# Transposing the normalized tiles by DMA from SBUF to SBUF instead of on TensorE, in a hybrid decoder trunk on eight cores

## The reference, cut to what matters

```
h    = rms_norm(x, norm_mix)                       # (B, S, 1024)
proj = h @ w_in                                    # 1024 -> 8192: b_a c_a u_a u_p q_x g_a g_p g_x
y_a  = (b_a * causal_dwconv3(c_a * u_a)) @ w_conv_out
y_p  = per_group_linear(trailing_mean(u_p; 2, 4, 8, 16) - u_p) * pool_scale
mem_n = rms_norm(mem, norm_mem)                    # 256 memory tokens
y_x  = cross_attention(q_x, mem_n @ w_kv) @ w_xattn_out
x    = x + (sigmoid(g_a)*y_a + sigmoid(g_p)*y_p + sigmoid(g_x)*y_x) @ w_out
h    = rms_norm(x, norm_ffn)
x    = x + (silu(h @ w_gate) * (h @ w_up)) @ w_down    # 1024 -> 2816 -> 1024
return rms_norm(x, norm_final)
```

## Time and profile before

| | us |
|---|---|
| median of 3 runs | 1241.22 (1235.62 to 1244.12) |
| span of the profiled execution, slowest core (core 5) | 1244.8 |
| the other cores of that execution | 1225.2 to 1235.6 |
| TensorE busy, of that span | 1166.6 (94%) |
| VectorE, ScalarE busy | 512.5 (41%), 298.8 (24%) |

### The profile page before, as it was taken

How to read it: one execution, slowest core, us unless ns; L and a number is a source line. 1 busy time by engine, 2 the same in 40 slices (tenths; PEclk the granted TensorE clock), 3 DMA queues, 4 the chain that set the end, 5 groups by cost and what they waited for, 6 DMA issues and landing times.

```text
span 1244.8 us, 14721 instructions; the slowest of 8 cores (1225.2 to 1244.8 us)
## 1 busy us (share of the span) xinstructions
PE 1166.6 (94%) x5720; PEld 536.8 (43%) x5720; DVE 512.5 (41%) x504; ACT 298.8 (24%) x412; POOL 132.0 (11%) x154
## 2 busy tenths in 40 slices
PE   2786999999999899999989999989999989999997
PEld 2342444444444444444444444434444444444443
DVE  4003679843334411211163378883333531121125
ACT  5322232211112511001164322221111341101112
POOL 2021111110010210021100001111101021002000
PEclk9988999999999999999989999999999999999999
DMA  9999655535468496059984355557554669009302
GB/s 241 133 133 127 84 68 68 68 43 67 63 83 203 71 145 81 1 86 135 144 212 114 46 68 68 68 68 86 63 63 60 172 99 171 10 1 138 40 17 119
DMA packets 164756, 115.95 MB, mean 93 GB/s; under 512 B 11456, under 2 KB 151872, under 8 KB 164688
## 3 DMA queue, kind: packets, MB, share of 16 engines
q0 software_dynamic: 156640, 85.50, 56.6%
q1 hardware_dynamic: 8048, 29.51, 6.7%
HBM read 192.10 MB, written 8.39 MB: 161 GB/s over the span
## 4 chain that ended last, share of the span: by engine, by line
PE 74%; DVE 10%; DMA 9%; issue 3%; ACT 2%; POOL 0%; another core or an unknown queue 0%; SPq 0%; DVEq 0%; ACTq 0%; POOLq 0%
PE ps L183 74%; DMA ring<-w_kv 4%; DMA ring<-w_in 3%; DVE rden L559 2%; DMA tmp<-x 1%; DMA arena<-x 1%; DVE tmp L475 1%; DVE tmp L478 1%; DVE tmp L509 1%; DVE tmp L513 1%; DVE tmp L468 1%; DVE arena L520 1%; DVE tmp L505 1%; ACT junk L263 1%; PE ps L278 1%
## 5 line engine op out<-in xcount | busy, mean ns | idle before, releaser
L183 PE MATMUL ps<-arena,ring 128*128 128x512 bf16 (+1 forms) x4160 | 878.8, 371 | 33.1 <-DMA ring<-w_in 18.4
L183 PEld LDWEIGHTS ps<-arena,ring 128*128 128x128 bf16 x4160 | 393.1, 98 | 510.0 <-issue 49.2
L719 DVE TENSOR_TENSOR arena<-ps,tmp 128x1024 bf16<-128x1024 f32 x44 | 53.9, 1224 | 254.5 <-PE ps L183 239.6
L183 PE MATMUL ps<-arena 128*128 128x512 bf16 x704 | 155.1, 382 | 1.6 <-DVE stat L267 1.6
L716 ACT ACTIVATE tmp<-ps 128x1024 f32<-128x1024 f32 x44 | 45.1, 1024 | 319.1 <-PE ps L183 319.0
L183 PEld LDWEIGHTS ps<-arena 128*128 128x128 bf16 x704 | 69.0, 98 | 85.1 <-issue 4.1
L176 POOL DMA_DIRECT2D ring<-w_in x64 | 56.0, 875 | 460.0 <-PE ps L183 409.9
L737 DVE TENSOR_TENSOR arena<-ps,arena 128x1024 f32<-128x1024 f32 x32 | 39.2, 1223 | 79.2 <-PE ps L183 79.2
L183 PE MATMUL ps<-ring,arena 128*128 128x512 bf16 x256 | 56.9, 379 | 0.0
L263 ACT ACTIVATE junk<-arena 128x1024 bf16<-128x1024 f32 x40 | 42.1, 1053 | 58.1 <-DVE stat L267 29.0
L559 DVE RECIPROCAL rden<-ps 128x512 f32<-128x512 f32 x16 | 53.6, 3348 | 0.1
(11 more groups left out here) (73 smaller groups left out, 619.7 us busy)
## 6 DMA issues: line engine op xcount, KB each, us to landing
ring<-w_in POOLq DMA_DIRECT2D x64, 512.0 KB, 9.1
arena<-w_down POOLq DMA_DIRECT2D x4, 2816.0 KB, 23.4
ring<-w_gate POOLq DMA_DIRECT2D x20, 512.0 KB, 23.4
ring<-w_up POOLq DMA_DIRECT2D x20, 512.0 KB, 22.7
arena<-x SPq DMA_DIRECT2D x4, 2048.0 KB, 13.4
out<-tmp SPq DMA_DIRECT2D x16, 512.0 KB, 2.8
arena<-x SPq DMA_DIRECT2D x8, 512.0 KB, 15.2
ring<-w_kv POOLq DMA_DIRECT2D x8, 512.0 KB, 43.9
```

The source lines that it names most:

```text
L183: ins = e.matmul(o, l, r, start=s0, stop=s1)
L719: dve(lambda e, u=u, sg=sg, c=c: e.tensor_tensor(out=actT[:, c, :], in0=PU[u][:, 0:TM], in1=sg[:, 0:TM], op=ALU.mult), reads=[("PU", u), ( ...
```

## The change

`transpose_tile` issues one DMA transpose from the norm's buffer `hb` to `hT` (or `memT`) on SyncE's queue. The TensorE transposes, the PSUM buffer that they took from the rotation of three, and the copies out of PSUM are gone. The places in program order of all 35 calls stay. `on_dve` no longer has an effect.

```diff
     def transpose_tile(src_bf, src_keys, rows, dstT, c0, dst_keys, on_dve=False):
-        m = next_pu()
-
-        def fn(e):
-            ins = None
-            for kc in range(KC):
-                ins = e.transpose(PTv[m][:, kc, 0:rows], src_bf[:rows, kc * P:(kc + 1) * P], ident[:rows, :rows])
-            return ins
-        plan.op("pe", fn, reads=src_keys + [("ident",)], writes=[("PU", m)])
-        if on_dve:
-            dve(lambda e: e.tensor_copy(out=dstT[:, :, c0:c0 + rows], in_=PTv[m][:, :, 0:rows]),
-                reads=[("PU", m)], writes=dst_keys)
-        else:
-            act(lambda e: e.activation(out=dstT[:, :, c0:c0 + rows], in_=PTv[m][:, :, 0:rows], func=AF.Copy),
-                reads=[("PU", m)], writes=dst_keys)
+        plan.op("sp", lambda e: e.dma_start_transpose(out=dstT[:, :, c0:c0 + rows], in_=src_bf[:rows, :]),
+                reads=src_keys, writes=dst_keys, dma=True)
```

## The result

The changed kernel takes **1309.98 us**, median of 4 runs (1308.29 to 1325.54), against 1240.4 us before (4 runs, 1235.62 to 1244.12): the ratio is 1.0594, with a 95% interval of 1.0525 to 1.0663. It is 70 us slower. The forecast was 1269 us in a range of 1240 to 1340: the direction and the range held, the size did not, +70 us where +28 was said. In the profile the slowest core (core 2) spans 1307.0 us, and the cores agree (1292.3 to 1307.0). Some executions of every version, the kernel before included, run longer while one die or both show a lower granted clock; ratios, medians and profiles here are of the others.

The account below looks back on a forecast made before the run. TensorE was taken as the bound almost everywhere, full DMA engines at the start. Startup 15, C streams 8.4 and A stream 4.9 sum to +28.3: 1273 against the profiled 1244.8, 1269 us as run median, range 1240 to 1340.

Parts of the forecast that it names:

- Direction and bound: Whole kernel: TensorE, busy 94%, bounds it almost everywhere except the DMA-full start; the change makes it slower, chance 0.75.
- The rival on the other side: C and A stream ends: freed TensorE goes straight on, 18.6 us less, 1223 us; chance 0.03.
- A tile alone: A transpose with nothing beside it lands in 2.8 us: 1.3 fixed plus 1.5 of engine time.
- C streams, +4.2 each: Each C stream's end: last tile lands in 7 us beside weight loads, +2.4, and lower clock after idling, +1.8.
- Startup, +15: Startup: 10.1 tiles at 1.5 us of engine time delay weight loads on full DMA engines, +15 us.
- A stream, +4.9: A stream of half 1: VectorE waits for `hb`, +3.4; last two tiles stand behind a store on SP, +1.5.
- Rival 3: Beside weight loads, 64 pieces per engine wait 0.7 us each: startup, C and A streams +109, 1350 us; chance 0.14.
- Rival 1: Transposes go nearly free: startup costs 0 to 7.5, C ends gain 1.6 each, 1246 us; chance 0.20.
- Rival 4: Everywhere, a tile's eight blocks go one after another, 10.4 us a tile: +218, 1459 us; chance 0.08.

Follow-up runs that it names:

- e1: Kernel before, with only the 16 tiles of the two C streams transposed by DMA: 1282.5 us, ratio 1.0319.
- e5: e1 with the first `w_down` load of each half held until the last transpose has landed: 1243.3 us, ratio 1.0011.
- e2: Kernel before, with only the 9 startup tiles and two memory tiles transposed by DMA: 1256.5 us, ratio 1.0113.
- e9: e3 with five `hb` buffers instead of four: 1246.4 us, ratio 1.0036.
- e3: Kernel before, with only the 8 tiles of the A stream of half 1 transposed by DMA: 1248.8 us (two runs), no ratio.
- e10: e2 with the first `w_kv` load held until all tiles of hT have landed: 1252.6 us, ratio 1.0086.
- e11: Kernel before, with the first seven tiles of each C stream by DMA and the `w_down` load held until the seventh has landed: 1242.7 us, ratio 1.0001.
- e7: e1 with the DMA transpose replaced by a plain copy of the tile in 256-byte pieces: 1284.5 us, ratio 1.0327.
- e8: e1 with the DMA transpose replaced by a plain copy in 2 KB rows to spare buffers: 1250.8 us, ratio 1.0074.

## Why the prediction was wrong, point by point

**Direction and bound: right.** TensorE was freed of 23.0 us and gained nothing from it, because each place ends with a hand-over, not with TensorE. The rival on the other side (1223 us) needed landings that no place had.

**A tile alone: right.** 2.8 us of landing was said; 2.7 to 2.8 us was measured in every quiet moment (e1, e5).

**C streams, +4.2 each: the step that failed,** measured +20.7 and +18.4. Two things in it were wrong. I took 7 us for the landing of the last tile as a value between 2.8 and 16.8, reading the x and gain loads by their bytes. But they go in rows of 4 KB, 8 packets per engine to 512 KB, and a tile goes in 66, of which 64 are of 256 bytes; where queues take turns packet by packet, a number of packets is what has to be carried over, not a size. And I followed the last tile alone ("the first seven tiles are transposed while the DMA engines are nearly idle"). The `w_down` load came out at 427.16 and the seventh tile at 427.6, so it met the flood (19.1 us), and the last tile stood behind it and behind a gain load in the same queue: it landed 24.2 us after its issue where 7 were said, and TensorE idled 26.5 us where 9 were said. The clock was part of it about as said, 1.5 us instead of 1.8; the row that the 1.8 came from stands behind two waits of 3.12 and 1.65 us, though, and not behind a long idle.

**Startup, +15: about the right size for the wrong reason,** +19.6 measured, +16.7 alone. The term was engine time of 1.5 us a tile that delays weights. e2 shows no wait for weights at all: hT is complete at 72 us, not near 60, and sets everything after it. The price of a tile there was 4.9 us in turns with weights, where I had 3 to 4. The engine time itself was 1.16 us with nothing beside it and 2.3 us as a mean over the kernel, where I had 1.5 for all. That +15 lies near +19.6 is luck.

**A stream, +4.9: half of it,** +10.3 measured. Both mechanisms were there (e9): VectorE's wait for `hb`, 4.9 us instead of 3.4, and the end behind the last stores, 5.7 instead of 1.5. The second holds some 2.6 us of lower clock (e3), which I had counted for the C streams only.

**The rivals.** Rival 3 (every small piece waits its turn, 0.14) had the mechanism, and the 66 packets per engine are its 64 pieces and two more. It had the price of a turn from the x loads, 0.7 us; for a piece of 256 bytes a turn took 0.21 us beside `w_down` and 0.07 beside other weights. Hence its +32 us per C stream stood against +20.7 and its +35 at the startup against +19.6. Rival 1 (nearly free, 0.20) is what e5 makes of the C streams. Rival 4, with 10.4 us for every tile, is refuted by the landings of 2.7 us. The Trainium skill ("VectorE: DVE Perf Modes", "The three transpose paths") gives 1309 ns for one block by DMA; the estimate of 10.5 us a tile, which took it eight times, does not hold here: the eight blocks of a tile landed together in 2.7 us. A single block was not run.

**What stays open.** In what order x, mem, weights and transposes would have to be issued for a startup that hides eight transposes wasn't tried beyond e10. Why a tile issued as the flood starts moves hardly a packet in the first microseconds is not shown. And e3, with two times, shows its +10.6 us by its stages only.

## What to carry to other kernels

A small DMA issued beside a running bulk load costs, in the main, its number of packets per engine times the turn of the other queue's packet, not its bytes: count the pieces of both, and look at what is issued in the microseconds around it and ahead of it in its own queue. Where a hand-over must be by DMA, hold the bulk load back until it has landed; e5 shows that this costs nothing when the load has slack. Look at TensorE's granted clock after the hand-over as well: in e11 it took back the 2 us that the hand-over had gained. Work taken from the busiest engine gives nothing where the end of the stage is a hand-over that becomes longer.

## What the runs showed of the hardware that I had not expected

- A DMA transpose from SBUF to SBUF was no slower than a plain copy in pieces of the same size: 2.8 us alone for 128 x 1024 bf16 in both (e1, e7), and 24 us in both beside `w_down`. A copy in rows of 2 KB takes 2.3 us alone (e8).
- It moves in 1,056 packets a tile (1,040 the copy in the same pieces, 144 the copy in 2 KB rows, from the queue's packets less those of the kernel before, divided by 16 tiles: 24,944, 24,688 and 10,352 less 8,048).
- The issue of a transpose on SP takes 1.23 us in quiet moments, and up to 10.8 us in the changed kernel (15.3 us in e1) when its queue is backed up. SP's nine issues at the startup take 45.96 us.
- TensorE's granted clock was 0.62 after waits of 2.2 and 1.4 us with 1 us of transposes between them (e11), and 0.50 after waits of 5.8 us (e5) and 26.5 us (changed kernel).
